# Column order by loads and stores in the second layer, and a scan stage with other engines and wider evictions

## The reference

```
h_lat = rmsnorm(x, norm_g[i]) * (1.0 + scale) + shift ; h_lat = to_col_major(h_lat, rows)
xb, gate = split(h @ w_in) ; xc = short_conv(xb, conv_w) + conv_b
r = sigmoid(xc @ w_r + b_r) ; i = sigmoid(xc @ w_i + b_i)          # both directions, 4 diagonal blocks
log_a = -8 * r * softplus(-lam) ; a = exp(log_a)
b = sqrt(-expm1(2 * log_a)) * (i * xc)
h_t = a_t * h_(t-1) + b_t                  # forward and backward; latent starts from the context's state
y = ((h_f + h_b) * silu(gate)) @ w_out ; y = from_col_major(y) ; x = x + gate1 * y
out = rmsnorm(x, final_g)
```

## Time and profile before

| what | us or share |
|---|---|
| median of three runs (lowest, highest) | 4956.19 (4954.5, 4961.49) |
| span of the profiled execution | 4959.2 |
| TensorE, VectorE, ScalarE, GpSimd busy, share of the span | 84%, 58%, 43%, 38% |
| norm stage of layer 1 | 3826 to 3915 |
| projection of layer 1 | 3915 to 4325 |
| scan stage, first operation to last | 4334.5 to 4746 |
| output stage | 4746 to 4959.2 |

### The profile page before, as it was taken

How to read it: one execution, slowest core, us unless ns; L and a number is a source line. 1 busy time by engine, 2 the same in 40 slices (tenths; PEclk the granted TensorE clock), 3 DMA queues, 4 the chain that set the end, 5 groups by cost and what they waited for, 6 DMA issues and landing times. The chain is left out here.

```text
span 4959.2 us, 83385 instructions
## 1 busy us (share of the span) xinstructions
PE 4174.3 (84%) x30756; PEld 3454.9 (70%) x30756; DVE 2868.1 (58%) x3373; ACT 2116.9 (43%) x3991; POOL 1895.1 (38%) x1256
## 2 busy tenths in 40 slices
PE   7599999999997888888888888866998599866659
PEld 2288888888885777777777777765887488754447
DVE  3244555545554777777777777754553623269854
ACT  4122222232323666666666666652111511177722
POOL 2212121212121766766676666752111522132322
PEclk8799999999998999999999999997999699977779
DMA  6212222222223444443444444434543221212134
GB/s 225 86 48 77 66 79 64 69 65 79 65 70 85 111 112 114 114 114 109 114 115 111 110 110 114 114 107 173 184 176 123 68 79 61 91 53 89 51 127 140
DMA packets 589093, 503.64 MB, mean 102 GB/s; under 512 B 115584, under 2 KB 557184, under 8 KB 575872
## 3 DMA queue, kind: packets, MB, share of 16 engines
q1 hardware_dynamic: 588960, 501.82, 33.3%
HBM read 351.00 MB, written 150.67 MB: 101 GB/s over the span
## 5 line engine op out<-in xcount | busy, mean ns | idle before, releaser
L551 PE MATMUL pj_bank<-h_hi,pj_whi 128*128 128x512 f32 (+1 forms) x1920 | 717.3, 374 | 21.8 <-POOL pj_wlo L537 19.1
L551 PE MATMUL pj_bank<-h_lo,pj_whi 128*128 128x512 f32 (+1 forms) x1920 | 708.0, 369 | 0.0
L551 PE MATMUL pj_bank<-h_hi,pj_wlo 128*128 128x512 f32 (+1 forms) x1920 | 707.7, 369 | 0.0
L741 ACT ACTIVATE pj_raw<-pj_bank 128x512 f32<-128x512 f32 (+1 forms) x240 | 128.1, 554 | 955.1 <-PE pj_bank L551 476.1
L534 POOL TENSOR_TENSOR pj_whi<-pj_w,ones 128x1024 fp32r<-128x1024 f32 x48 | 115.3, 2403 | 1024.1 <-PE pj_bank L551 1009.6
L551 PEld LDWEIGHTS pj_bank<-h_hi,pj_whi 128*128 128x128 f32 x1920 | 363.2, 189 | 87.0 <-POOL pj_wlo L537 19.6
L1364 DVE TENSOR_TENSOR dc_Y<-dc_psY,dc_pick 128x256 f16<-128x256 f32 x864 | 323.4, 415 | 170.9 <-PE dc_psY L1115 170.9
L1270 ACT ACTIVATE dc_R<-dc_psR 128x256 f16<-128x256 f32 x720 | 245.9, 382 | 400.6 <-PE dc_psR L1131 399.7
L551 PEld LDWEIGHTS pj_bank<-h_lo,pj_whi 128*128 128x128 f32 x1920 | 363.3, 189 | 62.8 <-issue 3.8
L551 PEld LDWEIGHTS pj_bank<-h_hi,pj_wlo 128*128 128x128 f32 x1920 | 362.9, 189 | 60.9
L834 DVE TENSOR_SCALAR pj_acc<-pj_raw,pj_conv_w 128x2307 f32<-128x2307 f32 x32 | 90.7, 2835 | 473.9 <-ACT pj_raw L741 473.9
(11 more groups left out here) (264 smaller groups left out, 10750.3 us busy)
## 6 DMA issues: line engine op xcount, KB each, us to landing
dc_tm<-scratch_tm SPq DMA_DIRECT2D x288, 192.0 KB, 2.5
dc_cgr<-scratch_cgrow SPq DMA_DIRECT2D x288, 128.0 KB, 2.8
dc_fm<-scratch_fm SPq DMA_DIRECT2D x288, 128.0 KB, 2.3
scratch_o<-dc_ob SPq DMA_DIRECT2D x288, 128.0 KB, 2.0
scratch_tm<-pj_tm SPq DMA_DIRECT2D x24, 1152.0 KB, 5.2
pj_w<-in_gdn_w_in SPq DMA_DIRECT2D x48, 512.0 KB, 6.3
scratch_fm<-pj_row SPq DMA_DIRECT2D x16, 1152.0 KB, 5.3
dc_kr<-scratch_fm SPq DMA_DIRECT2D x288, 64.0 KB, 2.6
```

The costliest lines, as they stand in the source:

```text
L551: i = pe.matmul(self.bank[blk][:, 0:n], l[b][:, k, :], r[:, k, at:at + n], start=(m == 0), stop=(m == 3 * KT - 1))
L741: act.activation(raw_row(raw, blk), pr.bank[blk][:, 0:BLKS[blk][1]], ACT.Silu if KINDS[j] == "z" else ACT.Copy).then_inc(pr.s_ev, 1)
```

## The change

Norm stage: each latent tile is loaded in column order, by four DMAs of 32 rows that lie 64 tokens (256 KB) apart in memory; context tiles take four DMAs too. `hi` and `lo` are written contiguously. Output stage: `mixed` is now in column order, so residual loads and output stores are four DMAs of 32 rows each, with the same distance.

Scan stage: GpSimd has no work. VectorE takes I times input (`gated_input`) and the whole `lo` part of the input. The square of a is ScalarE's second exp (`nc16`). Eight banks become four pairs, and a unit's gates have 3 groups each (256, 1024, 1024 columns). VectorE's product with the gate is contiguous. The next block's `lo` parts are made at u%4 = 3 and no longer at u%4 = 2.

```diff
@@ phase_norm
-        place = ... strided view of buf for column order; hsplit likewise
+        place = lambda buf, i: buf[:, :, i * P:(i + 1) * P]
+            latent = src[CTX:TOK, :].rearrange("(r c) d -> c r d", c=GRID_W)
+            return [(p, latent[(i - CCH) * COLS + c]) for c, p in enumerate(parts)]
-                    sp.dma_start(xt[i % XB][:], src[i * P:(i + 1) * P, :]).then_inc(load[i % XB], 16)
+                    for p, rows in rows_of(i):
+                        sp.dma_start(xt[i % XB][p, :], rows).then_inc(load[i % XB], 16)
@@ phase_scan
+    PARTS = [(0, CTX), (CTX, 1024), (CTX + 1024, 1024)]
-        bank = [... [P, 512] ... for i in range(8)]
+        bank = [... [P, 1024] ... for i in range(4)]
-        GR = [(g, blk) for g in range(2) for blk in range(NB)]
+        GR = [(g, part) for g in range(2) for part in range(len(PARTS))]
-                                if not (first and n < 8):
-                                    pe.wait_ge(s["ev"], b * (4 * NG) + n - 7)
+                                if not (first and n < 4):
+                                    pe.wait_ge(s["ev"], b * (4 * NG) + n - 3)
...
                     act.activation(Tn[d][:], A[d][:], ACT.Tanh, ...)
+                    act.activation(V[:], A[d][:], ACT.Exp, scale=nc16[:, d, row:row + 1]).then_inc(s["sq"], 1)
...
+                def gated_input(u, b, t, d):
+                    dve.wait_ge(s["ev"], (u + 1) * NG)
+                    dve.tensor_tensor(I[d][:], I[d][:], xc[b % 2][:, t], ALU.mult).then_inc(s["ix"], 1)
...
-                    dve.tensor_tensor(mixed[:].rearrange("p (r c) -> p c r", c=GRID_W), ...
+                    dve.tensor_tensor(mixed[:], H[0][:, CTX:TOK], gate[:], ALU.mult).then_inc(s["mix"], 1)
                 for u, b, t, d in units:
+                    gated_input(u, b, t, d)
                     if u:
                         scan(u - 1, 1 - d)
-                    dve.wait_ge(s["a"], u + 1)
-                    dve.tensor_tensor(V[:], A[d][:], A[d][:], ALU.mult).then_inc(s["sq"], 1)
...
-                    if u % 4 == 2 and b + 1 < LB:
+                    if u % 4 == 3 and b + 1 < LB:
                         split(b + 1)
@@ phase_output_lru
-                    sp.dma_start(xt[j][:], dram["tokens1"][bass.ds(at + CTX, P), :]).then_inc(load_x[j], 16)
+                    src = columns(dram["tokens1"][CTX:TOK, :])[bass.ds(at, COLS)]
+                    for c in range(COLS):
+                        sp.dma_start(xt[j][c * ROWS:(c + 1) * ROWS, :], src[c]).then_inc(load_x[j], 16)
```

More of the change, by code:

```diff
@@ L153, in phase_norm @@
         sem = head_semaphores(nc, T)
+    COLS = P // ROWS
+    PARTS = COLS if col_major else 1
     HALF = 3 * D // 2
@@ L175, in phase_norm, with rows_of @@
         ctx_of = lambda i: 1 if i < CCH else 0
[L177 to L186, removed]
+        place = lambda buf, i: buf[:, :, i * P:(i + 1) * P]
+        def rows_of(i):
+            if not col_major:
+                return [(slice(0, P), src[i * P:(i + 1) * P, :])]
+            parts = [slice(c * ROWS, (c + 1) * ROWS) for c in range(COLS)]
+            if i < CCH:
+                return [(p, src[i * P + p.start:i * P + p.stop, :]) for p in parts]
+            latent = src[CTX:TOK, :].rearrange("(r c) d -> c r d", c=GRID_W)
+            return [(p, latent[(i - CCH) * COLS + c]) for c, p in enumerate(parts)]
         def turns(*steps):
@@ L1768, in phase_scan @@
         br, bi = sb("br", [P, 2, KT]), sb("bi", [P, 2, KT])
[L1769 to L1773, removed]
+        lam, tl = sb("lam", [P, 2, KT]), sb("tl", [P, 2, KT])
+        c8, nc8, nc16 = sb("c8", [P, 2, KT]), sb("nc8", [P, 2, KT]), sb("nc16", [P, 2, KT])
+        bank = [ctx.enter_context(nc.psum_tensor(f"sc_b{i}", [P, 1024], F32)) for i in range(4)]
+        names = ("const", "la", "le", "ln", "lp", "lq", "rates", "w_hi", "w_lo", "x_hi", "x_lo", "mm", "ev", "tanh",
+                 "sq", "a", "v", "root", "ix", "b", "scan", "ctx_scan", "sum", "mix", "gate_load", "stored")
         s = {q: sem("sc_" + q) for q in names}
         load_w, load_x = ([sem(f"sc_{x}{j}") for j in range(2)] for x in ("load_w", "load_x"))
-        GR = [(g, blk) for g in range(2) for blk in range(NB)]
+        GR = [(g, part) for g in range(2) for part in range(len(PARTS))]
         NG = len(GR)
@@ L1811, in _ @@
                 sp.wait_ge(s["stored"], 16 * KT)
[L1813 to L1823, removed]
             @block.tensor
@@ L1833, in one @@
                         for d in range(2):
-                            for g, blk in GR:
-                                if not (first and n < 8):
-                                    pe.wait_ge(s["ev"], b * (4 * NG) + n - 7)
[L1837 to L1843, removed]
+                            for g, part in GR:
+                                if not (first and n < 4):
+                                    pe.wait_ge(s["ev"], b * (4 * NG) + n - 3)
+                                at, w = PARTS[part]
+                                for h in range(0, w, 512):
+                                    n512 = min(512, w)
+                                    m = 0
+                                    for l, r in ((whi, xhi), (whi, xlo), (wlo, xhi)):
+                                        for k in range(2):
+                                            i = pe.matmul(bank[n % 4][:, h:h + n512], l[:, d, g, k, t * P:(t + 1) * P],
+                                                          r[:, k, at + h:at + h + n512], start=(m == 0), stop=(m == 5))
+                                            m += 1
                                 i.then_inc(s["mm"], 1)
                                 n += 1
-                assert 4 * NG % 8 == 0
+                assert 4 * NG % 4 == 0
                 one(0, True)
@@ L1858, in split @@
                     act.wait_ge(load_x[b % 2], 16 * (b // 2 + 1))
-                    for k in range(2):
+                    for k in range(S2):
                         act.activation(xhi[:, k], xc[b % 2][:, k], ACT.Copy).then_inc(s["x_hi"], 1)
```

56 lines of the change are left out of this document (30 added, 26 removed).

## The result

The changed kernel takes 4984.65 us (4 runs, 4978.43 to 4988.97) where the kernel before takes 4955.34 in the same comparison (4953.15 to 4961.49). The ratio is 1.0056 with a 95% interval of 1.0043 to 1.0069, so about 28 us more, with an interval of 21 to 34 (the two medians lie 29.3 apart). The prediction was 4974, slower, with the range 4950 to 4996. Direction and place were right; the loss was forecast as 17.6 us and is 27.8, and the interval doesn't reach down to the forecast.

What follows compares the result with a forecast made beforehand. ScalarE's cycle was taken to set plain scan units, late `lo` parts the block starts, TensorE the output stage. Norm -16, scan +31.6 and output +2 gave +17.6 on 4956.2, so 4974 us, range 4950 to 4996.

Steps and rivals of the forecast that it cites:

- Norm stage: Norm stage: contiguous writes shorten turns and tail, less late loads; -16 us, between -13 and -17.
- Rival C: Norm and output loads: DMAs of 32 rows are slow through ports or pitch; +35 to +42 in sum, 4995 us; 12%.
- GpSimd no longer behind: Norm stage's tail: only the last `lo` write stands at the end, saving another 2 x 2.38 us at most.
- VectorE not the bound: Scan stage: VectorE needs 17.0 us per unit, while ScalarE's work makes a unit 21.7.
- near 75% busy: Scan stage, a sign to look for: VectorE's busy share near 75%.
- ScalarE's cycle: Scan stage, plain unit: 12.8 us of ScalarE work between evictions plus 8.9 of evictions, 21.7 in all.
- I take 9 at 1.2 GHz: Scan stage evictions: 9 matmuls per unit run at the lower TensorE clock, adding 1.9 us.
- Rival A: Scan stage: TensorE doesn't fall back to 1.2 GHz, or only briefly; evictions 7.0, in sum -11, 4945 us; 10%.
- rival B: Scan stage: VectorE's 17.0 sets the pace, bank pairs let TensorE run far enough ahead; 4885 us; 3%.
- D's "5 to 6 a unit": Scan stage: few matmuls at 1.2 GHz and a slightly shorter chain; +4 to +9, 4963 us; 15%.
- Block start: Scan stage, new block: TensorE starts 27.3 us after the last eviction, nothing hides it; step 42.8, three times.
- The stage's sum: Scan stage: 443.1 us against 411.5, +31.6; +3 to +44 by the eviction bounds used.

Runs made afterwards that it cites:

- the column-order experiment: The kernel before with only column-order loads and stores in the norm and output stages and the contiguous gate product, scan stage otherwise as before: 4939.14 us, ratio 0.9955.
- The seven banks with their filling: Changed kernel with split at u%4 = 2 and seven single banks, plus 24 unread matmuls per unit except a block's first: 4894.26 us; without those matmuls 4909.43.
- the kernel with the small part last: Changed kernel with split at u%4 = 2, eight single banks, and each gate's 256 context columns last instead of first: 4880.27 us, ratio 0.9833 to the kernel before.

## Why the prediction was right, and where its sizes were off

**Norm stage: -16 forecast, -12.5 measured.** The turns came as said, 3.36. From the first square to the last it is 57.2 in place of 65.7, -8.5 where the steps gave -11.2 + 0.6 + 1.0 = -9.6: the waits for loads took 3.3, not 1.6, two of the three at the start. Rival C is out: four parts of 32 rows land after a median of 2.7 each, the first tile is complete 4.1 us after its first issue (3.1 to 4.9 was the forecast), and turns in the middle have no wait. One tile per turn is 512 KB in 3.36 us, 156 GB/s; a limit above that couldn't show here. The tail fell by 4.0 and not 6.2. The term "GpSimd no longer behind" is the one that was wrong: GpSimd still works without a pause to the end, four writes in 11.31, and the middle two take 3.40 and 3.33 where the outer ones take 2.37 and 2.33. Both overlap an addition of VectorE with both inputs in SBUF (L250). The first addition started 0.03 us before GpSimd's write, took its own 1.22, and the write came after it; the second started 1.0 before the write ahead of it ended, and took 2.12. It is what the column-order experiment showed: the two don't run at once. The prediction had counted no such wait. The range given, -13 to -17, was a little too narrow.

**VectorE not the bound: right.** It needs 17.0 per unit by the sum (16.9 in the row below), and plain units have 22.3. That ScalarE has no more waits for `sc_H` was said and is so. The sign "near 75% busy" was an error of arithmetic: 4 x 17.0 = 68 against 3 x 21.7 + 42.8 = 107.9 is 63%, and this row of one block has 67.65 of 109.4, 62%:

```profile
4400.00:4509.40 109.40, 58.69 (x240) 48.02 (x240) 67.65 (x28) 76.56 (x56) 0.00 (x0) 0.75 0.19 70
```

**ScalarE's cycle: mechanism right, one term too small.** Forecast 12.8 + 8.9 = 21.7, measured 12.7 + 9.6 = 22.3. The step "I take 9 at 1.2 GHz" is the one mis-sized: 8 of the 12 units have 12 or 13 such matmuls and 4 have 7 or 8. In a unit with 12 the 24 matmuls take 4474.13 - 4465.98 = 8.15, in one with 8 4386.53 - 4379.39 = 7.14, where 7.4 was taken. The mean over the twelve is 7.81, 0.4 more. The rest of the 0.7 is small links: 0.52 from the first eviction's start to TensorE's, not 0.35; 0.2 to the last eviction, not 0.1; the eviction itself 1.12, not 1.05. Eleven times 0.6 is 6.6. The seven banks with their filling show that the clock is no mere reading of the trace. Rival A (no fall of the clock) and rival B (TensorE far enough ahead) are out, and D's "5 to 6 a unit" too.

**Block start: 42.8 forecast, 42.2 measured**, three times 0.6 less. Its mechanism is shown by the split put back, 15.5 each.

**The stage's sum.** +31.6 was forecast and +38.0 measured. The 6.4 between them: plain units +6.6, block starts -1.7, unit 0 to 1 19.4 and not 18.2, +1.2, and the two ends +0.3.

**Output stage: +2 forecast, +2.2 measured.** TensorE is still full there, to be read against the earlier trace rows:

```profile
4796.00:4972.00 176.00, 175.75 (x768) 145.10 (x768) 62.88 (x73) 36.14 (x60) 40.99 (x16) 0.99 0.47 129
```

The changed stages and the projection add up to -12.5 - 0.4 + 38.0 + 2.2 = 27.3, and the ratio says 27.8 (the two spans differ by 23.0, since the part before them was 4.3 shorter in that execution). What the change has to give is greater than what it loses: with its two harmful parts out, it is worth 64 us. Column order alone gives 22 of these. The other 42 (46.7 by the scan stage) came with GpSimd taken out of the stage and its work given to VectorE; in the kernel before VectorE's operations beside GpSimd are long throughout (`wlo` at 4426.61 takes 7.10 where it takes 2.28 in the changed kernel, the product at 4401.47 4.18 and not 2.56). In the two settings where it was tested the exp isn't what gives the gain, but a kernel before with GpSimd's work moved and nothing else was not run, so the 42 are not shown alone.

## What to carry to other kernels

Before merging PSUM banks for fewer, wider evictions, count the columns that can lie ready while the evicting engine does something else: here the engine saved 0.4 us per unit (2.36 + 0.48 + 2 x 1.12 = 5.1 of evictions without waits, beside 5.5 in the kernel with the small part last) and then waited 4.5 (9.6 less 5.1) for the columns that found no bank, computed at 1.2 GHz in part, since TensorE had been idle without a free bank. What a stage's next round waits for belongs ahead of its engine's remaining work on the current round, as soon as its input is there. And a long VectorE operation is to be read beside GpSimd's row before its access pattern is blamed.

## What the runs showed of the hardware that was not expected

- A contiguous VectorE product of 2.29 us took 7.16 beside one GpSimd multiplication and ended 2.15 after it; GpSimd's took 6.47 there, where it had started beside VectorE's sum, and 5.16 where it started alone.
- TensorE came back at 1.2 GHz after 4.21, 5.68 and 7.49 us of idle time and at 2.4 after 0.26. After 3.07 it came back at 2.4 and fell to 1.2 after about three matmuls, in the midst of work (0.73, 0.78, 1.05 for two). And with seven banks it came back at 1.2 after only 2.40 (at 4356.44), so the length of the last idle time alone doesn't tell the clock. Rows of the kernel with the small part last:

```profile
4400.88 0.73 PE L1828 MATMUL sc_b<-sc_xhi,sc_whi 128*128 128x512 f32 x2 [3.07 <-ACT sc_A L1869]
4401.44 0.78 PE L1828 MATMUL sc_b<-sc_xlo,sc_whi 128*128 128x512 f32 x2
4402.02 1.05 PE L1828 MATMUL sc_b<-sc_xhi,sc_wlo 128*128 128x512 f32 x2
...
4443.78 1.22 PE L1828 MATMUL sc_b<-sc_xhi,sc_whi 128*128 128x512 f32 x2 [4.21 <-ACT sc_A L1869]
```

- Work that nobody reads made a kernel faster: 24 matmuls per unit, 12 times, gave 19 us by the ratios and 17.9 by the scan stage.
- Four DMAs of 32 rows that lie 256 KB apart bring a tile fast enough for a turn of 3.36 us, but for 3.3 us of waits in the stage: each lands after 2.7 us, beside 3.7 for one DMA of 128 contiguous rows.
